# Two-layer hybrid decoder on one core: the output projection's operand turned in 32x32 blocks by VectorE and re-partitioned through DRAM instead of transposed by TensorE, and two gate blocks exchanged

## What is computed

```python
(aq, ak, av, ag, su, sv, sg, mq, mk, mv, mo, mg, mi, mf) = split_columns(x @ w_in)
att = ...                                   # dilated attention, 256 x 512
sgu = spatial_gating(gelu(su), gelu(sv), ...)  # 256 x 512
h = mlstm_chunkwise(...) * sigmoid(mo)      # 256 x 1024, four heads of 256
ml = head_norm(h, head_norm_g)
mix = concatenate([att * silu(ag), sgu * silu(sg), ml * silu(mg)], axis=-1)
x = layer_norm(alpha * x + mix @ w_out, ln_g, ln_b)
```

## Time and profile before

| | |
|---|---|
| median of 3 runs | 1271.83 us (1271.44 to 1271.86) |
| profiled execution, span | 1269.9 us |
| TensorE, matmuls | 1257.0 us busy, 99% |
| VectorE | 893.0 us, 70% |
| ScalarE | 705.4 us, 56% |
| GpSimd | 244.0 us, 19% |
| granted TensorE clock, mean | 0.997 of full speed |
| DMA | 264.97 MB, 209 GB/s over the span |

### The profile page before, as it was taken

How to read it: one execution, slowest core, us unless ns; L and a number is a source line. 1 busy time by engine, 2 the same in 40 slices (tenths; PEclk the granted TensorE clock), 3 DMA queues, 4 the chain that set the end, 5 groups by cost and what they waited for, 6 DMA issues and landing times.

```text
span 1269.9 us, 16388 instructions
## 1 busy us (share of the span) xinstructions
PE 1257.0 (99%) x6342; PEld 1040.2 (82%) x6342; DVE 893.0 (70%) x1229; ACT 705.4 (56%) x989; POOL 244.0 (19%) x268
## 2 busy tenths in 40 slices
PE   9999999999999999999999999999999999999996
PEld 8888888878888888888888788888888888888885
DVE  5686876876667655865785779768665776567656
ACT  5477476575555544444563775666755555345441
POOL 0321522522220000400003223334131200004000
PEclk9999999999999999999999999999999999999998
DMA  9968768765665555465657587678546556565562
GB/s 336 310 209 261 236 189 277 260 192 164 204 195 174 184 186 185 152 230 190 207 186 238 183 282 245 193 258 282 184 149 215 183 157 209 165 197 198 186 212 86
DMA packets 129277, 264.97 MB, mean 209 GB/s; under 512 B 8824, under 2 KB 8976, under 8 KB 128688
## 3 DMA queue, kind: packets, MB, share of 16 engines
q1 hardware_dynamic: 123712, 247.23, 60.6%
q0 software_dynamic: 3680, 13.28, 3.0%
q10 hardware_dynamic: 1808, 3.42, 0.7%
HBM read 258.61 MB, written 5.28 MB: 208 GB/s over the span
## 4 chain that ended last, share of the span: by engine, by line
PE 86%; ACT 4%; DVE 4%; POOL 3%; issue 2%; DVEq 0%; POOLq 0%; ACTq 0%
PE ps L373 79%; ACT arena L810 2%; DVE w_lo L1060 2%; ACT w_hi L736 2%; PE ps L444 1%; PE ps L671 1%; PE ps L391 1%; PE ps L639 1%; POOL arena L1684 1%; PE ps L533 0%; POOL arena L1680 0%; PE ps L518 0%; ACT arena L807 0%; PE ps L355 0%; DVE arena L1133 0%
## 5 line engine op out<-in xcount | busy, mean ns | idle before, releaser
L1060 DVE TENSOR_TENSOR w_lo<-w_raw,w_hi 128x1024 fp32r<-128x1024 f32 x408 | 527.1, 1305 | 326.4 <-ACT w_hi L736 324.5
L736 ACT ACTIVATE w_hi<-w_raw 128x1024 fp32r<-128x1024 f32 x408 | 427.3, 1058 | 388.9 <-PE ps L373 339.3
L373 PE MATMUL ps<-w_hi,xT_hi 128*128 128x512 f32 x1616 | 636.2, 394 | 0.7 <-DVE w_lo L1060 0.7
L373 PE MATMUL ps<-w_hi,xT_lo 128*128 128x512 f32 x1616 | 629.6, 390 | 0.0
L373 PE MATMUL ps<-w_lo,xT_hi 128*128 128x512 f32 x1616 | 629.0, 389 | 0.0
L373 PEld LDWEIGHTS ps<-w_hi,xT_hi 128*128 128x128 f32 x1616 | 303.4, 188 | 64.3 <-issue 1.3
L373 PEld LDWEIGHTS ps<-w_hi,xT_lo 128*128 128x128 f32 x1616 | 303.3, 188 | 64.0
L373 PEld LDWEIGHTS ps<-w_lo,xT_hi 128*128 128x128 f32 x1616 | 303.6, 188 | 61.4
L292 POOL TENSOR_TENSOR carried<-ident 1x1 f32<-1x1 f32 x30 | 19.6, 652 | 454.8 <-DVE arena L1416 178.7
L1217 DVE CUSTOM_DVE_ANT_0 mix<-xres,mix 128x1024 f32<-128x1024 f32 x64 | 89.0, 1390 | 1.1
L807 ACT ACTIVATE arena<-arena 32x256 f32<-32x256 f32 x128 | 53.2, 416 | 15.6 <-DVE arena L1137 14.0
(11 more groups left out here) (244 smaller groups left out, 825.3 us busy)
## 6 DMA issues: line engine op xcount, KB each, us to landing
w_raw<-w_in_dram SPq DMA_DIRECT2D x367, 512.0 KB, 4.5
w_raw<-w_out_dram SPq DMA_DIRECT2D x64, 512.0 KB, 4.8
mix<-gate_w_dram SPq DMA_DIRECT2D x32, 512.0 KB, 5.6
xres<-x_dram ACTq DMA_DIRECT2D x4, 512.0 KB, 8.4
v_dram<-arena POOLq DMA_DIRECT2D x4, 512.0 KB, 6.3
z<-v_dram POOLq DMA_DIRECT2D x8, 256.0 KB, 5.6
z<-ln_g_dram POOLq DMA_DIRECT2D x2, 1024.0 KB, 7.7
store<-ln_b_dram POOLq DMA_DIRECT2D x2, 1024.0 KB, 7.9
```

The source lines that it names most:

```text
L373: mm = pe.matmul(ps[2 * s + t][:], a[:, order[c] * KC + k, t * P:(t + 1) * P], b[:, k], start=(c + k + i == 0), stop=(c == CH - 1 and k == ...
L736: A(hi_of(n, c), w_raw[:, c % RING], ACT.Copy).then_inc(w_hi_done, 1)
L1060: TTn(lo_of(n, c), w_raw[:, c % RING], hi_of(n, c).bitcast(F32), ALU.subtract).then_inc(w_lo_done, 1)
```

## The change

The transposes on TensorE are gone. In their place each of the four parts of the mixed tile (attention, SGU, first and second half of the mLSTM, 512 features each) takes this way:

1. VectorE turns it: one block transpose of 128x1024, 32x32 blocks at a time (`turn_mix`), from `mix` into a part of `arena` that is no longer needed.
2. SP writes it to a DRAM scratch, 512 KB in pieces of 128 values (`put`), and once that has landed fetches it back in four DMAs, one for each group of 32 partitions (`fetch`), so that the blocks come to stand on the right partitions.
3. ScalarE copies hi and VectorE subtracts lo, 128x1024 at a time; the second mLSTM half in two pieces of 128x512 (`operand`).

Puts and fetches stand between weight loads on SP's queue at fixed places (`puts`, `fetches`: behind which chunk's load). The SGU gate block takes the place of the mLSTM gate block and the other way round, and the output projection takes its features in plain order, so that the second mLSTM half comes last. GpSimd multiplies the first half's gate by the gain early, and after the head norm only the second half by its gain; VectorE does both products of head and gate. GpSimd's two LayerNorm DMAs wait for the attention operand's lo and for the second half's product.

```diff
-N_SU, N_SV, N_CONV, N_MV, N_MG1, N_SG, N_OUT = 13, 14, 15, 19, 21, 22, 23
+N_SU, N_SV, N_CONV, N_MV, N_SG, N_MG1, N_OUT = 13, 14, 15, 19, 21, 22, 23
...
-OUT_ORDER = (0, 1, 4, 5, 6, 7, 2, 3)
+ATT, SGU, ML_A, ML_B = range(PARTS)
+TURN_ORDER = (ATT, ML_A, SGU, ML_B)
+STEPS = PARTS + 1
+QUARTER = P // 4
...
+        mix_zT = [arena[:, at:at + 1024] for at in (0, 2048, 1024, 4096)]
+        mix_T = [z[:, 0].rearrange("p t c -> p (t c)")] + [arena[:, at:at + 1024] for at in (6144, 3072, 5120)]
...
+        mix_dram = nc.dram_tensor("mix_dram", (DEPTH, PARTS, 4, TT, 4, QUARTER, P), F32, kind="Internal").ap()
...
+        def step(l, c):
+            return l * STEPS + (c // 2 + 1 if c < CH - 1 else STEPS)
...
+                def put(p):
+
+                    sp.wait_ge(mix_turned, l * PARTS + TURN_ORDER.index(p) + 1)
+                    dst = mix_dram[l, p].rearrange("f t u j x -> (u j) (f t) x")
+                    sp.dma_start(dst, mix_zT[p].rearrange("p (a x) -> p a x", a=4 * TT)).then_inc(mix_put[p], 16)
+
+                def fetch(p):
+
+                    sp.wait_ge(mix_put[p], (l + 1) * 16)
+                    src = mix_dram[l, p].rearrange("f t u j x -> f j (t u) x")
+                    dst = mix_T[p].rearrange("p (b x) -> p b x", b=SEQ // QUARTER)
+                    for f in range(4):
+                        sp.dma_start(dst[f * QUARTER:(f + 1) * QUARTER], src[f]).then_inc(mix_moved[p], 16)
...
-                for i in range(D // BW):
-                    load(w_out, N_OUT + i, i * BW, OUT_ORDER)
+                load(w_in, N_MG1, (MG + 1) * BW, plain, puts={0: ATT, 6: ML_A, 7: SGU}, fetches={2: ATT})
+                load(w_out, N_OUT, 0, plain, puts={7: ML_B}, fetches={0: ML_A, 1: SGU})
+                load(w_out, N_OUT + 1, BW, plain, fetches={0: ML_B})
+                load(w_out, N_OUT + 2, 2 * BW, plain)
+                load(w_out, N_OUT + 3, 3 * BW, plain)
...
-                chunks(N_MG1, Q_MG1, 0, 5, CH)
-
-
-                chunks(N_SG, Q_SG, 1, 0, 4)
-                transposes(mix, CH, OUT_ORDER, 0, ((h_done, (l + 1) * MH), (mix_att, l + 1)))
-                transposes(mix, CH, OUT_ORDER, 1)
-                chunks(N_SG, Q_SG, 1, 4, CH)
...
+                chunks(N_SG, Q_SG, 0, 5, CH)
+
+                chunks(N_MG1, Q_MG1, 1, 0, CH)
+
+                for c in range(CH):
+                    pe.wait_ge(mixT_lo, step(l, c))
+                    chunks(N_OUT, Q_OUT, 0, c, c + 1)
...
+                def operand(p, j=0, n=PART_TILES):
+
+                    act.wait_ge(mix_moved[p], (l + 1) * 4 * 16)
+                    act.wait_ge(w_used, used(l, N_MG1, 2 * p + 1))
+                    A(mix_target(xT_hi, p, j, n), mix_source(p, j, n), ACT.Copy).then_inc(mixT_hi, 1)
...
+                split(N_MG1, 4, 6)
+                operand(ATT)
+                split(N_MG1, 6, 8)
+                split(N_OUT, 0, 2)
+                operand(SGU)
+                split(N_OUT, 2, 4)
                 act.wait_ge(w_used, used(l, N_OUT, -1))
...
+                A(mix[:, 0, 3 * BW:4 * BW], ps[2][:], ACT.Silu)
+                A(mix[:, 1, 3 * BW:4 * BW], ps[3][:], ACT.Silu).then_inc(z_act, 1)
+                operand(ML_A)
+                split(N_OUT, 4, 8)
+                operand(ML_B, 0, KC)
+                operand(ML_B, KC, KC)
...
+                def turn_mix(p):
+
+                    V.transpose(mix_zT[p].rearrange("p (f b s) -> p b f s", f=4, b=TT * PART_TILES),
+                                mix[:, :, p * BW:(p + 1) * BW]).then_inc(mix_turned, 1)
```

More of the change, by code:

```diff
@@ L300, in _, with load @@
             for l in range(DEPTH):
-                def load(w, n, col, order, gate=()):
+                def put(p):
[8 more added lines that the diff above has]
+                        sp.dma_start(dst[f * QUARTER:(f + 1) * QUARTER], src[f]).then_inc(mix_moved[p], 16)
+                def load(w, n, col, order, gate=(), puts={}, fetches={}):
                     for c in range(CH):
@@ L327, in load @@
                                      ).then_inc(w_landed[c % RING], 16)
+                        if c in puts:
+                            put(puts[c])
+                        if c in fetches:
+                            fetch(fetches[c])
                 plain = tuple(range(CH))
@@ L378, in chunks @@
                             mm.then_inc(done, 1)
[L380 to L393, removed]
                 def unit(l, i):
@@ L446, in by_product @@
                     mm.then_inc(w_used, 1)
-                def first_block(n, q, src, first, order, u0, ready):
-                    for u in range(u0, 4):
-                        transposes(src, first, order, u, ready.get(u, ()))
-                    for c in range(CH):
-                        pe.wait_ge(xt_lo, mix_first(l) + c + 1)
-                        chunks(n, q, 0, c, c + 1, order)
-                        if c + 4 < CH:
-                            transposes(src, first, order, c + 4, ready.get(c + 4, ()))
                 if l == 0:
@@ L746, in affine @@
                     f.then_inc(xa_hi, 1)
-                def operand(n, c0, first, order, u0=0, u1=CH):
-                    for u in range(u0, u1):
-                        if u >= c0:
-                            split(n, u, u + 1)
-                        act.wait_ge(xt_ps, mix_first(l) + u + 1)
-                        A(xT_hi[:, order[u] * KC:(order[u] + 1) * KC, :],
-                          ps[4 + u % 4][:].rearrange("p (k t) -> p k t", k=KC), ACT.Copy).then_inc(xt_hi, 1)
+                def operand(p, j=0, n=PART_TILES):
+                    act.wait_ge(mix_moved[p], (l + 1) * 4 * 16)
+                    act.wait_ge(w_used, used(l, N_MG1, 2 * p + 1))
+                    A(mix_target(xT_hi, p, j, n), mix_source(p, j, n), ACT.Copy).then_inc(mixT_hi, 1)
                 if l == 0:
@@ L1074, in affine, with operand @@
                     f.then_inc(xt_lo, 1)
[L1076 to L1085 removed]
+                def operand(p, at, j=0, n=PART_TILES):
+                    dve.wait_ge(mixT_hi, l * STEPS + at + 1)
+                    TTn(mix_target(xT_lo, p, j, n), mix_source(p, j, n), mix_target(xT_hi, p, j, n).bitcast(F32),
+                        ALU.subtract).then_inc(mixT_lo, 1)
+                def turn_mix(p):
+                    V.transpose(mix_zT[p].rearrange("p (f b s) -> p b f s", f=4, b=TT * PART_TILES),
+                                mix[:, :, p * BW:(p + 1) * BW]).then_inc(mix_turned, 1)
                 def take(n, s, dst):
```

139 lines of the change are left out of this document (72 added, 67 removed).

## The result

The changed kernel takes **1287.95 us** (median; 1286.02 to 1289.38) against 1271.82 for the kernel before: a ratio of 1.0127, 95% interval 1.0113 to 1.0141. It is 1.3% slower. The forecast was 1266.5, the range 1264.0 to 1274.5, so the prediction was wrong in sign and the time lies outside its range.

The account below looks back on a forecast made before the run. TensorE's issued work was taken as the bound: span 1269.9 less 7.36 us of transposes gives 1262.5, plus 1.9 from span to median gives 1264.5, plus 2.0 us of waits before chunk 6 gives 1266.5 us; range 1264.0 to 1274.5.

Parts of the forecast that it names:

- What is removed: TensorE, both layers: 64 transposes go, which hold 3.68 us a layer, 7.36 us in both.
- nothing waits: First rival: the whole round trip is hidden and TensorE waits for nothing new; 1264.5 us, chance 0.22.
- Gate blocks and VectorE: Exchanging gate blocks costs nothing; VectorE's turns (1.24 us) and products (1.22) meet mLSTM gate chunk 4 with 0.7 us slack.
- The fourth rival: Turns queue with GpSimd's products, so TensorE waits 1.7 us a layer at mLSTM gate chunk 4; 1267.9 us, chance 0.05.
- The step that failed: Second mLSTM half's round trip before output chunk 6: there at 557.7, 1.0 us late a layer, 2.0 in both.
- P: Time of SP's put of the second mLSTM half to DRAM: 3.5 us, from rows of 2.7 and 6.3.
- F: Time of the fetch of the second mLSTM half back from DRAM: 5.1 us, from rows of 3.4 to 7.9.
- The SGU fetch "lands at about 540": SGU part's fetch, beside the LayerNorm gain, priced at a load's 7.9 us; it makes the mLSTM SiLUs 2.0 us later.
- The second rival: LayerNorm bias transfer meets the second mLSTM half's fetch: 3.8 us late a layer, 7.6 in both; 1272.1 us, chance 0.20.
- The clock: Forecast is wrong if the granted clock falls behind TensorE's wait before chunk 6; no size given.
- the third: Third rival: 512 B runs slow puts (6.3 us) and fetches (7.9); 6.6 us late a layer, 1277.7 us, chance 0.15.
- 0.65 for faster: Chance that the whole kernel gets faster: 0.38 forecast, 0.22 nothing waits, 0.05 fourth rival; same 0.20, slower 0.15.

Follow-up runs that it names:

- Without the trip: Changed kernel with the scratch puts and fetches left out, operands made straight from VectorE's turned data (output not the reference's): 1264.8 us, ratio 0.9946.
- The version that gains 0.37%: Changed kernel with both LayerNorm transfers late, ML_B's trip started and fetched earlier, ML_A's chunks before SGU's, ML_B's operands before chunk 7's split: 1267.01 us.
- the early order alone: Changed kernel with ML_B's SiLUs, product, turn, put and fetch moved earlier, both LayerNorm transfers where the change has them: 1276.72 us, ratio 1.0046.
- both transfers late: Changed kernel with GpSimd's LayerNorm gain and bias transfers both waiting until every output projection operand is done: 1273.82 us, ratio 1.0022.
- ML_A's chunks first: Changed kernel with both LayerNorm transfers late, ML_B's trip started early and fetched behind the seventh load, ML_A's chunks before SGU's: 1272.98 us, ratio 1.0009.

## Why the prediction was wrong, point by point

**What is removed: right.** Without the trip the time was 1264.8; the prediction had 1264.5 for "nothing waits".

**Gate blocks and VectorE: right.** The turn takes 1.25 us (predicted 1.24), the product 1.23 (1.22), one split stands behind GpSimd's product, and TensorE does not wait at the gate block's chunk 4. VectorE after:

```profile
522.02 1.25 DVE L1094 STREAM_TRANSPOSE arena<-mix 128x1024 f32<-128x1024 f32 x1
523.18 2.31 DVE L1070 TENSOR_TENSOR w_lo<-w_raw,w_hi 128x1024 fp32r<-128x1024 f32 x1
```

GpSimd ran its two products from 520.80 to 524.41. The turn ran beside them at full speed, the split with its two inputs took 2.31 instead of 1.23. The fourth rival (the turns queue) falls. The Trainium skill ("SBUF — State Buffer", section "Who interferes with whom") says that a VectorE instruction with one SBUF input does not contend with GpSimd and one with two does, and these rows agree with it.

**The step that failed** is the start and the put of ML_B. The prediction's sum: product done at 546.0, put at 547.4, P = 3.5, F = 5.1, operands 1.7, so 557.7. Measured: the put at 553.30 (5.9 later), P = 7.40 (+3.9), from the first fetch issue to the last landing 4.0 (-1.1), operands 1.4 (-0.3): 557.7 + 5.9 + 3.9 - 1.1 - 0.3 = 566.1, where TensorE went on. Two terms were mis-sized, and both stand beside a LayerNorm transfer; between them in the list is one that had no price at all:

- *The SGU fetch "lands at about 540".* I priced it by a weight load beside the bias transfer, 7.9. It landed at 533.7 + 12.3 = 546.0. One load beside 1 MB was the wrong model: here two fetches, the loads held up behind SyncE's puts, and the gain all stood in the queue together. Even without the gain it took 8.2.
- *The weight loads of chunks 2 and 3*, which the prediction took to be there. Issued at 534.2 and 535.0 into the same jam, they landed at 547.1 and 548.5, 12.9 and 13.6 us later. ML_B's SiLUs stood behind the fetch and both splits, and it is the load of chunk 3 that stands in the chain: a fetch that landed at 540, with the loads as late as they were, would not have brought the SiLUs forward.
- *P = 3.5.* The rows gave 2.7 to 6.3, and I took SP's own undisturbed write. The second rival saw the bias transfer leave behind the product, but let it meet the fetch. It left at 552.21, ahead of the put at 553.30, and it held the put: 7.4, outside both ends. By the time of the fetch it was over (552.21 + 7.0 = 559.2), so F came out better than forecast.

**A wait not listed.** TensorE stood for 4.0 and 3.0 us before chunk 2. The prediction used the late SGU operand only as a delay for ML_B; landing at 546.0 it misses its own deadline of 545.8, and the split of chunk 2 stands behind it. That split's own weights, issued at 534.23, were later still (547.1), so that either would have made the wait:

```profile
DMA to landing us min/median/max: 12.9/12.9/12.9
```

**The clock.** That it could fall was named and not priced. It costs 2.6 us, behind the last wait. With 9.5 in layer 1 (566.1 - 556.6) that leaves about 10 for layer 2: 1284.9 - 1262.8 (the span without the trip) = 22.1 = 9.5 + 10.0 + 2.6.

**The rivals.** The outcome is nearest to the third (slower, 1277.7), but its mechanism is at most a part: where the queue was free, a put in 512-byte runs took 3.2 and 3.4 us and a part of a fetch 2.7. Per byte the short runs do cost more. A put of this kind (first line, now) and the output's write in 4 KB runs (second line, before) both fill the DMA engines, the one at 289 GB/s, the other at 406:

```profile
524.50:525.50 1.00, 1.00 (x6) 0.83 (x5) 1.00 (x2) 1.00 (x2) 0.00 (x0) 1.00 1.04 289
```

```profile
1267.30:1268.30 1.00, 0.00 (x0) 0.00 (x0) 0.00 (x0) 0.00 (x0) 0.00 (x0) 0.50 1.02 406
```

How much of the jam is due to that, no run shows: a trip in longer runs was not tried.

The rule that stood beside this rival, of the Trainium skill ("VectorE: DVE Perf Modes", section "Rules for kernel authors": TensorE for a 128x128 transpose), agrees with the change as made, which lost 1.3%. The version that gains 0.37% with the same turns and the same way through DRAM shows that the rule does not decide it here; the neighbours of the trip do.

**Chances.** 0.65 for faster rested on prices taken from calmer stretches, one transfer at a time. The stretch from 534 to 545 was 83% busy before; the change puts 1.5 MB of puts and as much of fetches into this neighbourhood in each layer, and moves the gain's 1 MB from 482 to 532, while the bias goes on from 534.6 to 552. Adding up bytes alone would not have shown it: from 530 to 545 the changed kernel moves 263 GB/s, no more than the kernel before (268), but its DMA share there is 1.08 instead of 0.76. Without the trip it is 0.88, at 313 GB/s.

## What to carry to other kernels

Price a new DMA round trip by everything that is queued in its stretch, in the time that it takes of the DMA engines and not in bytes alone, large transfers of other queues first, and look where each of those starts once the change has moved it. On engines that work in order, put the instructions that start the longest trip ahead of those that wait for another one, and the operand that is needed first ahead of the load that is needed next. A wait or a slow clock ahead of a later, longer wait costs nothing, so removing it gains nothing until the later one is gone, unless the same step also brings the later one forward, as moving the gain did (5.6 us).

## What the runs showed of the hardware that was not expected

ML_B's put, a 512 KB write by SyncE's queue, took 7.4 to 8.4 us beside a 1 MB broadcast that GpSimd had issued 1.1 us earlier, in four kernels; in a fifth, with the early order alone, it took 11.1 and 9.9. Without the broadcast it took 3.9 to 5.7 in seven. Cutting the broadcast's packets from 8 KB to 2 KB did not change that (8.0 and 7.6).

The clock did not follow the length of one idle alone. It fell to 1.2 GHz behind idles of 3.98 and 5.47 us and stayed at 2.4 GHz behind 2.92 and 2.97. But with both transfers late it fell behind 2.21 (0.66 from 560 to 565),

```profile
560.00:565.00 5.00, 5.00 (x16) 3.91 (x16) 2.80 (x3) 2.36 (x3) 1.29 (x3) 0.66 0.99 360
```

and with ML_A's chunks first it stayed behind 2.37:

```profile
560.00:565.00 5.00, 4.90 (x21) 4.05 (x22) 3.61 (x5) 2.20 (x3) 2.21 (x3) 1.00 0.73 219
```

What tells them apart is open, and it is not the kernel alone: with both transfers late, the ten executions took 1272.87 to 1276.74 us, and the three longest (the profiled one is the longest) are those with a mean granted clock of 0.994 or 0.995, against 0.996 or 0.997 in the others.
